# A 256-token hybrid transformer on one core: a leaner preparation, and one activation moved from the sigmoids to the exponentials

## What is computed

```python
for layer in range(2):
    hdn = swiglu(rmsnorm(x, ng[0]), ffn1...);  x = x + 0.5 * rmsnorm(hdn, ng[1])
    hdn = rmsnorm(x, ng[2])
    hdn = nsa_ssd_mixer(hdn, ...) if layer == 0 else rwkv7_time_mix(hdn, ...)
    x = x + rmsnorm(hdn, ng[3])
    hdn = swiglu(rmsnorm(x, ng[4]), ffn2...);  x = x + 0.5 * rmsnorm(hdn, ng[5])
```

```python
w = -softplus(-(w0 + tanh(xw @ w1) @ w2)) - 0.5      # decay
a = sigmoid(a0 + (xa @ a1) @ a2)                     # the second small projection
k = k * (1 + (a - 1) * k_a)                          # the key correction
decay = exp(-exp(w));  kk = normalised k * k_k
```

## Time and profile before

| | |
|---|---|
| median of 3 runs | 2081.16 us (2075.07, 2081.16, 2082.08) |
| the profiled execution | 2079.93 us, its span (first to last instruction) 2078.1 us |
| mean granted TensorE clock | 0.929 |
| busy: PE, PE weight loads, DVE, ACT, POOL | 92%, 68%, 27%, 18%, 3% of the span |
| bytes moved | 232 MB |

### The profile page before, as it was taken

The page is one execution under the profiler, slowest core; times in us unless marked ns, Lnnn a source line. Parts: engine busy times, 40 slices in busy tenths (PEclk is TensorE's granted clock), DMA queues, the critical chain, the costliest instruction groups (busy, mean ns, idle before and its releaser), DMA issues.

```text
span 2078.1 us, 21581 instructions
## 1 busy us (share of the span) xinstructions
PE 1920.3 (92%) x8569; PEld 1406.6 (68%) x8569; DVE 555.1 (27%) x1334; ACT 383.4 (18%) x964; POOL 56.7 (3%) x68
## 2 busy tenths in 40 slices
PE   6999989789669999999998899989999899999998
PEld 4767678667536777677776676857777667737774
DVE  1000111633331000110005485730000343613344
ACT  1000110133111000110002542220000244312431
POOL 0200000000000000000000032100000000000000
PEclk9999999855579999999999996999999999999999
DMA  6754624210013444434453331025355774466630
GB/s 203 231 171 133 170 85 132 91 41 1 0 41 122 147 157 151 164 110 163 141 166 97 115 120 38 20 81 162 126 177 124 96 123 83 80 104 82 104 100 21
DMA packets 190869, 232.21 MB, mean 112 GB/s; under 512 B 22868, under 2 KB 172696, under 8 KB 190792
## 3 DMA queue, kind: packets, MB, share of 16 engines
q1 hardware_dynamic: 188032, 223.85, 39.5%
q0 software_dynamic: 1840, 5.12, 0.8%
q10 hardware_dynamic: 920, 2.16, 0.3%
HBM read 230.07 MB, written 1.05 MB: 111 GB/s over the span
## 4 chain that ended last, share of the span: by engine, by line
PE 66%; DVE 3%; ACT 1%; issue 1%; DVEq 0%
PE ps L504 22%; PE ps L277 17%; PE ps L522 10%; PE ps L461 5%; PE ps L1572 1%; PE ps L1407 1%; PE ps L545 1%; PE ps L2091 1%; PE ps L2107 1%; PE ps L360 1%; PE ps L2095 1%; PE ps L2121 1%; PE ps L2126 1%; PE ps L1589 1%; PE ps L1601 0%
## 5 line engine op out<-in xcount | busy, mean ns | idle before, releaser
L504 PE MATMUL ps<-hT,ring 128*128 128x256 f32 x2816 | 625.0, 380 | 4.0 <-issue 4.0
L504 PEld LDWEIGHTS ps<-hT,ring 128*128 128x128 f32 x2816 | 537.6, 191 | 111.9 <-issue 42.6
L277 PE MATMUL ps<-hT,ring 128*128 128x272 f32 (+3 forms) x1408 | 336.6, 394 | 5.5 <-issue 3.2
L277 PEld LDWEIGHTS ps<-hT,ring 128*128 128x128 f32 (+2 forms) x1408 | 257.3, 186 | 67.8 <-issue 11.9
L522 PE MATMUL ps<-ring,arena 128*128 128x512 f32 x640 | 287.7, 592 | 0.0
L576 DVE TENSOR_TENSOR arena<-arena,ps 128x256 f32<-128x256 f32 x88 | 37.1, 422 | 854.9 <-ACT arena L561 854.9
L522 PEld LDWEIGHTS ps<-ring,arena 128*128 128x128 f32 x640 | 121.6, 190 | 118.9 <-issue 114.8
L561 ACT ACTIVATE arena<-ps 128x256 f32<-128x256 f32 x88 | 33.7, 383 | 849.4 <-PE ps L504 849.4
L461 PE MATMUL ps<-ring,arena 128*128 128x512 f32 (+1 forms) x256 | 112.6, 596 | 1.4 <-ACT arena L2156 0.8
L277 PE MATMUL ps<-arena 128*128 128x64 f32 (+6 forms) x384 | 98.8, 421 | 15.0 <-DVE arena L1264 12.7
L277 PEld LDWEIGHTS ps<-arena 128*128 128x128 f32 (+2 forms) x384 | 78.4, 291 | 31.4 <-DVE arena L1264 14.8
(11 more groups left out here) (366 smaller groups left out, 1571.7 us busy)
## 6 DMA issues: line engine op xcount, KB each, us to landing
ring<-in_ffn_w_gate SPq DMA_DIRECT2D x44, 1024.0 KB, 5.3
ring<-in_ffn_w_up SPq DMA_DIRECT2D x44, 1024.0 KB, 5.3
ring<-in_ffn_w_down SPq DMA_DIRECT2D x44, 1024.0 KB, 5.0
ring<-in_w_in SPq DMA_DIRECT2D x32, 1024.0 KB, 11.3
ring<-in_ab_w_in SPq DMA_DIRECT2D x13, 1024.0 KB, 5.4
ring<-in_w_out SPq DMA_DIRECT2D x8, 1024.0 KB, 5.0
ring<-in_ab_w_out SPq DMA_DIRECT2D x6, 1024.0 KB, 4.8
ring<-in_c_w_k SPq DMA_DIRECT2D x4, 1024.0 KB, 5.4
```

What stands on the lines that cost most here:

```text
L277: last = nc.tensor.matmul(o, l, r, start=(i == 0), stop=(i == len(pairs) - 1))
L504: m = nc.tensor.matmul(ps[:, 4 + j % 2, 256 * w:256 * (w + 1)], slot8(s0 + 3 * q + w)[:, k, c * P:(c + 1) * P], hT[:, k, META:], start=(k ...
```

## The change

In the preparation: (1) x, in two halves, and the identity with the epsilons (the first 132 columns of the reordered constants, 66 KB) are issued by SP, ahead of the weights. (2) ACT's stream starts with the 8 rows of the first norm's gains, then the other 18 small loads, and the rest of the constants comes last. (3) PE transposes the first 8 rows alone and DVE copies them; the other rows are transposed by `columns_pe` behind x's own transposes, and copied by `columns_dve` behind `hT`'s emptying. The barriers `step_end` are gone. PE, ACT and DVE wait for x, the identity and, where they need them, the columns; the rest of the constants (`const_in`) is waited for ahead of the first mixer. In the time-mixing layer: (4) the activation into `MB[2][:, j]` and the wait before it leave the sigmoid loop; the activation is now the first instruction of `decays(j)`, ahead of its wait for `c_ready`, and DVE waits for it (`am_ready`) ahead of L1819.

```diff
@@ CONST @@
-for _name, _n in (("ident", P), ("rot", P), ... ("sin", L2), ("pairsel", 2), ("eps", 4)):
+for _name, _n in (("ident", P), ("eps", 4), ("rot", P), ... ("sin", L2), ("pairsel", 2)):
+NEARLY = P + 4
@@ trans_act / trans_dve @@
+            act.wait_ge(col_in, 1 if post is None else 2)
             lo = META
...
+                if post is not None:
+                    dve.wait_ge(col_in, 2)
@@ first_loads @@
-            for t in range(T):
-                load(x[:, t, :], d["x"][0, t * P:(t + 1) * P, :])
-            load(cst[:, :], d["consts"])
+            eng.dma_start(rowsA[0:8, :], rows(d["norm_gains"][0, 0])).then_inc(row_in, 16)
             for i, (l, g) in enumerate((l, g) for l in range(2) for g in (0, 2, 4)):
-                load(rowsA[8 * i:8 * i + 8, :], rows(d["norm_gains"][l, g]))
+                if i > 0:
+                    load(rowsA[8 * i:8 * i + 8, :], rows(d["norm_gains"][l, g]))
...
             load(pe_rows[32:64, :], d["a_cmp_pe_v"][0])
+            eng.dma_start(cst[:, NEARLY:], d["consts"][:, NEARLY:]).then_inc(const_in, 16)
@@ prep_pe, prep_act, prep_dve @@
         def prep_pe(pe):
+            pe.wait_ge(ident_in, 16)
+            pe.wait_ge(row_in, 16)
+            nc.tensor.transpose(ps[:, 7, 0:8], rowsA[0:8, :], ident[0:8, 0:8]).then_inc(row_t, 1)
+
+        def columns_pe(pe):
             pe.wait_ge(first_in, 16 * n_first.n)
-            (three transposes to bank 0; pe_end(pe) twice)
+            pe.wait_ge(col_in, 1)
+            (the three transposes, to bank 7).then_inc(rows_t, 1)
         def prep_act(act):
-            act.wait_ge(first_in, 16 * n_first.n)
-            act_end(act)
-            act_end(act)
+            act.wait_ge(x_in, 16 * T)
+            act.wait_ge(ident_in, 16)
         def prep_dve(dve):
-            dve.wait_ge(first_in, 16 * n_first.n)
-            dve_end(dve)
-            (three copies from bank 0; dve_end(dve))
+            dve.wait_ge(x_in, 16 * T)
+            dve.wait_ge(row_t, 1)
+            nc.vector.tensor_copy(colA[:, 0:8], ps[:, 7, 0:8]).then_inc(col_in, 1)
+            dve.wait_ge(col_in, 1)
+        def columns_dve(dve):
+            dve.wait_ge(rows_t, 1)
+            (three copies from bank 7, the last .then_inc(col_in, 1))
@@ rwkv_act @@
             def decays(j):
+                act.wait_ge(act_out, job["sig", j, 1])
+                nc.scalar.activation(MB[2][:, j, :], w_a[:, j, :], ACT.Identity, scale=colB[:, 72 + j:73 + j],
+                                     bias=kfix[:, j:j + 1]).then_inc(am_ready, 1)
                 act.wait_ge(c_ready, j + 1)
...
-                alink(act, nc.scalar.activation(w_a[:, j, :], next_a()[:, 0:S], ACT.Sigmoid, bias=colB[:, 56 + j:57 + j]))
-                nc.scalar.activation(MB[2][:, j, :], w_a[:, j, :], ACT.Identity, scale=colB[:, 72 + j:73 + j],
-                                     bias=kfix[:, j:j + 1]).then_inc(act_out, 1)
+                nc.scalar.activation(w_a[:, j, :], next_a()[:, 0:S], ACT.Sigmoid, bias=colB[:, 56 + j:57 + j]).then_inc(act_out, 1)
@@ rwkv_dve @@
                     nc.vector.tensor_tensor(w_ep[:, j, :], w_c[:, j, :], w_ep[:, j, :], ALU.subtract).then_inc(c_ready, 1)
+                    dve.wait_ge(am_ready, j + 1)
                     nc.vector.tensor_tensor(w_k[:, j, :], MB[2][:, j, :], w_k[:, j, :], ALU.mult).then_inc(kp_ready, 1)
@@ the engines' programs @@
             prep_pe(pe)
             trans_pe(pe)
+            columns_pe(pe)
...
             trans_dve(dve, colA[:, 0:8], None)
+            columns_dve(dve)
...
+                    (pe, act, dve).wait_ge(const_in, 16)      # behind the wait for later_in, layer 0
...
         def _(sp):
+            for t in range(T):
+                sp.dma_start(x[:, t, :], d["x"][0, t * P:(t + 1) * P, :]).then_inc(x_in, 16)
+            sp.dma_start(cst[:, 0:NEARLY], d["consts"][:, 0:NEARLY]).then_inc(ident_in, 16)
```

More of the change, by code:

```diff
@@ L41 @@
 _at = 0
-for _name, _n in (("ident", P), ("rot", P), ("blockones", P), ("ones", P), ("upper", P), ("strict", P), ("upper2", P),
+for _name, _n in (("ident", P), ("eps", 4), ("rot", P), ("blockones", P), ("ones", P), ("upper", P), ("strict", P), ("upper2", P),
                   ("qmask", L2), ("segmask", P), ("cmpadd", T * NCMP),
-                  ("cmpmul", T * NCMP), ("cos", L2), ("sin", L2), ("pairsel", 2), ("eps", 4)):
+                  ("cmpmul", T * NCMP), ("cos", L2), ("sin", L2), ("pairsel", 2)):
     CONST[_name] = (_at, _n)
@@ L225, in model_kernel @@
         w2k, w2v = small[0:64, 192:320], small[0:64, 320:384]
-        first_in = sem("first_in")
+        x_in, ident_in, first_in, const_in = sem("x_in"), sem("ident_in"), sem("first_in"), sem("const_in")
         later_in = sem("later_in")
@@ L641, in later_loads @@
             load(xm[:, :], d["meta_tokens_2"])
+        row_in, row_t, col_in, rows_t = sem("row_in"), sem("row_t"), sem("col_in"), sem("rows_t")
         def prep_pe(pe):
+            pe.wait_ge(ident_in, 16)
+            pe.wait_ge(row_in, 16)
+            nc.tensor.transpose(ps[:, 7, 0:8], rowsA[0:8, :], ident[0:8, 0:8]).then_inc(row_t, 1)
+        def columns_pe(pe):
             pe.wait_ge(first_in, 16 * n_first.n)
[L645 to L649, removed]
+            pe.wait_ge(col_in, 1)
+            nc.tensor.transpose(ps[:, 7, 0:NROW_A], rowsA, ident[0:NROW_A, 0:NROW_A])
+            nc.tensor.transpose(ps[:, 7, P:P + NROW_B], rowsB, ident[0:NROW_B, 0:NROW_B])
+            nc.tensor.transpose(ps[0:64, 7, 256:320], pe_rows, ident[0:64, 0:64]).then_inc(rows_t, 1)
         def prep_act(act):
-            act.wait_ge(first_in, 16 * n_first.n)
-            act_end(act)
-            act_end(act)
+            act.wait_ge(x_in, 16 * T)
+            act.wait_ge(ident_in, 16)
         def prep_dve(dve):
-            dve.wait_ge(first_in, 16 * n_first.n)
-            dve_end(dve)
[L659 to L662, removed]
+            dve.wait_ge(x_in, 16 * T)
[4 more added lines that the diff above has]
+            dve.wait_ge(rows_t, 1)
+            nc.vector.tensor_copy(colA[:, 8:NROW_A], ps[:, 7, 8:NROW_A])
+            nc.vector.tensor_copy(colB[:, :], ps[:, 7, P:P + NROW_B])
+            nc.vector.tensor_copy(small[0:64, 128:192], ps[0:64, 7, 256:320]).then_inc(col_in, 1)
         sc_ready, sc_masked, exp_done, p_ready = sem("sc_ready"), sem("sc_masked"), sem("exp_done"), sem("p_ready")
@@ L1358, in model_kernel @@
         c_ready, e_done, ax_ready, kp_ready, krr = sem("c_ready"), sem("e_done"), sem("ax_ready"), sem("kp_ready"), sem("krr")
-        kfix_in = sem("kfix_in")
+        kfix_in, am_ready = sem("kfix_in"), sem("am_ready")
         h_zero, t_zero, tt_zero, x_out = sem("h_zero"), sem("t_zero"), sem("tt_zero"), sem("x_out")
@@ L2302, in _ @@
                     pe.wait_ge(later_in, 16 * n_later.n)
+                    pe.wait_ge(const_in, 16)
                 if layer == 0:
@@ L2329, in _ @@
                     act.wait_ge(later_in, 16 * n_later.n)
+                    act.wait_ge(const_in, 16)
                 trans_act(act, colA[:, c + 8:c + 16], 0.5)
@@ L2354, in _ @@
                     dve.wait_ge(later_in, 16 * n_later.n)
+                    dve.wait_ge(const_in, 16)
                 trans_dve(dve, colA[:, c + 8:c + 16], 0.5, 3 * layer)
```

## The result

The changed kernel takes 2120.1 us (median of 6, 2103.9 to 2121.8) against 2078.8 for the one before: a ratio of 1.019 (1.016 to 1.022). I had forecast 2078.2, with 2070 to 2085 as the range. It is 41 us slower.

A forecast was written before the change was run, and what follows sets the result against it. PE was taken to bound the kernel, so an edit counts only where PE waits for it. Start -7.2 us and time-mixing layer +4.2 us gave -3.0 us: 2078.2 us on the median, range 2070 to 2085.

The forecast's parts named there:

- The start: Preparation up to the first feed-forward product: table load at 9.0, product from 24.54 to 17.4, a gain of 7.2 us.
- rival 3: Preparation: x lands no earlier for being first, start gains only ACT's 1.7 us of issues, 2083.7 us; chance 0.08.
- The layer: Time-mixing layer up to pair_scores(3): 4.2 us slower, from 2.7 of later pair_scores(3) and 1.5 of clock.
- I charged one fall with 1.5 us: Clock fall at PE's wait ahead of pair_scores(0): 2.0 us on r4, of which 0.5 has slack, leaving 1.5.
- rival 2: Time-mixing layer: the clock falls at both waits, ahead of pair_scores(0) and (1), 2.8 us more, 2081.0; chance 0.14.
- the sum: Time-mixing layer: step-by-step times by which DVE waits for ACT's moved activation, with pair_scores(0) at 1192.4 and (1) at 1204.7.
- so all of it goes through: Behind pair_scores(3): DVE's long solve and PE's v products start there, so its 2.7 us delay passes on whole.
- Rival 4: Time-mixing layer: clock falls ahead of pair_scores(0), not back before g1 ends; up to 24 us more, 2102; chance 0.05.
- I had charged 2.0: Clock loss on r4 from PE's wait of 4 to 6 us ahead of pair_scores(0), before 0.5 us of slack.

The follow-up runs named there:

- front_only: The changed kernel with the time-mixing layer as in the kernel before, so only the preparation differs from the kernel before: 2073.0 us, ratio 0.997.
- ahead_dense1: The changed kernel with the moved activation issued one block ahead and one added full-row product in the last g2 product: median 2089.9 us, 2065.2 to 2100.1.
- after_gap2: The changed kernel with two unused 256-wide DVE products directly ahead of the copies PE waits for (L1864): 2083.5 us, ratio 1.0013.

## Why the prediction was wrong

**The start was right**: table load 9.27 for 9.0, first product 17.38 for 17.4, gain 7.2; front_only confirms it in the total. But the gain isn't x's place ahead of the weights. In the kernel before, x stood first in ACT's queue, and that queue had moved 1.03 MB by 7.5 us and 1.22 by 8.05; so x (1.05 MB) was in by about 8 us, and ACT's issues let the table load start at 9.27 at the earliest. What went is the wait for the constants and the small loads, up to 15.54, with the two barriers. So rival 3 had its price wrong as well: by these figures the start would have gained its 7 us with x landing no earlier. The Trainium skill (DMA: Bandwidth & Descriptors, Issuing engines are not separate DMA queues) has transfers from different engines interleave on the same 16. The trace agrees: by 7.5 us SP's queue had moved 0.83 MB beside the 1.03 of ACT's.

**The layer was right in mechanism and too small in size**: 7.8 for 4.2. The sigmoids took 0.7 us more than 6.0. pair_scores(0) came 18.6 us behind the first sigmoid (18 forecast), (1) 14.6 behind (0) for 12.3 and 1.5 of clock, (3) 4.0 behind g1 for 3.5. What was mis-sized is above all the clock: I charged one fall with 1.5 us, and it fell around both waits, at 1181.6 and 1198.7, as my rival 2 had it, and again at 1219.2. r4 and r5 took 8.99, r6 and r7 8.86 where 7.17 is full speed, 1.8 and 1.7 us more (not 2.8), and pair_scores(0) 0.9 more. DVE's waits for ACT at blocks 0 and 3 stood where the sum put them; that at block 5, of 4.47, lay beside r6 and r7, as it had it.

**The step that failed** is the sentence "so all of it goes through": I took everything behind pair_scores(3) for a fixed length. The chunk stage isn't one: it took 57.4 us before and 96.0 in the changed kernel, with half the clock all through. That is 38.7 of the 42 us by which the forecast missed; the layer has the rest. The profile of before showed the clock back at 1301 in its front, after 41 us at half, and I didn't ask what brought it back. Rival 4 had the mechanism (half the clock that doesn't come back) at the wrong place, between pair_scores(0) and g1, at 0.05, and at most 24 us; there it came back each time, at 1188.5 and 1202.1, in the r products. Its other half, the mixer's stretch at 0.52 with PE 83% busy, was the right warning: a busy PE with small products is no guarantee of the clock. The Trainium skill (TensorE: Matmul & The Clock Gate, What's actually happening) has activity release the throttle; here PE's records cover all of 97 us and the granted clock stayed at half, so that sentence alone wouldn't have told which way this stage goes.

Open: why the front of the stage brings the clock back at one place in time and not at another, and what stays behind the spread of ahead_dense1. Delays of other sizes were not tried, and the changed kernel's one execution at 2103.9 has no trace; its mean granted clock was 0.918, where the other five had 0.907 to 0.911.

## What to carry to other kernels

Where a stage of small products sits between two clock levels, its length isn't a constant that a shift leaves alone: find each place in the trace where the clock comes back, and ask what did it and by how little. Judge an edit with the stages behind it on both levels, and test a suspect result with a pure delay, at a place that the critical engine waits at. And a step moved down one engine's program is paid by whoever needs it: run it one block ahead of its use.

## What the runs showed of the hardware

- The clock's place in time repeats with the program: in before, front_only and after_gap2 it came back 40.96 us after it fell, and in six kernels the stage's fate went with its distance from the fall, alike to 0.15 us within either group. Outside of these two distances no rule was found.
- The chunk stage took 57.4 us with the clock at full after its first 4 us, and 96.0 at half throughout, a ratio of 1.67 and not 2: at the full clock PE waits for DVE (3.5 us for L1889), and some 4 us more are not accounted for. Where the clock moved in its middle the length lay between.
- Around a wait of PE of 5.4 us the clock fell, and the products behind it took 2.7 us more (1.8 + 0.9), where I had charged 2.0. Around one of 3.6 us it fell again, for 1.7 us more.
